# Splitting two more output-gate tiles and interleaving half gate tiles with the attention units of a two-layer hybrid decoder step

## What is computed

```python
h = rmsnorm(x)
hq, hf, hi, hg, nq, kc, vc, ks, vs, kw, vw, ngate, mgate = jnp.split(h @ w_in, splits, axis=-1)
o_hg = hgrn2(hq, hf, hi) * silu(hg)                       # 4 heads, gated by hg
q = rope(nq)                                              # 8 heads of 64, 2 KV groups
o_cmp, o_slc = nsa_cmp_slc(q, ...)                        # compressed blocks, selected blocks
o_win = window(q, ...)                                    # sliding window
o_nsa = g[:, :, 0] * o_cmp + g[:, :, 1] * o_slc + g[:, :, 2] * o_win
mg = sigmoid(mgate)                                       # two merge gates of 1024 channels
x = x + (mg_a * (o_hg @ W_a) + mg_b * (o_nsa @ W_b)) @ w_out
x = x + (gelu(causal_conv3(h2 @ W_gate)) * (h2 @ W_up)) @ W_down,   h2 = rmsnorm(x)
```

## Time and profile before

| | |
|---|---|
| median of 3 runs | 1149.6 us (1146.79 to 1154.12) |
| profiled execution, its own time | 1147.22 us |
| its span | 1145.4 us (1.8 us less than its time) |
| mean granted clock | 0.983 |
| the stage in layer 0 | 143.7 to 244.2 us of the span |
| the same in layer 1 | 699.8 to 800.3 us |

### The profile page before, as it was taken

One profiled execution on the slowest core, in us unless ns is written; L12 is line 12 of the kernel. 1 busy time (PEld: TensorE's weight loads), 2 busy tenths in 40 slices (PEclk: granted clock), 3 DMA queues, 4 the chain that ended last, 5 costly groups with the idle time before them and its releaser, 6 DMA issues.

```text
span 1145.4 us, 21244 instructions
## 1 busy us (share of the span) xinstructions
PE 1111.0 (97%) x8581; PEld 1030.6 (90%) x8581; DVE 726.4 (63%) x1303; ACT 540.3 (47%) x865; POOL 293.0 (26%) x428
## 2 busy tenths in 40 slices
PE   6999999999999999999999999999999999999997
PEld 5988767778999999999999787777899999999996
DVE  5797166557567777763478845565756677777443
ACT  4543265554356555542454335654534555555332
POOL 2156453423121000000024572622311211000002
PEclk8999989999999999999999999899999999999998
DMA  9565322347644444345455635212784444443321
GB/s 295 154 166 207 111 84 75 111 119 221 223 147 148 148 147 148 113 139 170 148 120 197 200 94 164 74 38 76 221 268 148 147 152 154 154 132 120 134 81 47
DMA packets 151752, 165.94 MB, mean 145 GB/s; under 512 B 31596, under 2 KB 114406, under 8 KB 151398
## 3 DMA queue, kind: packets, MB, share of 16 engines
q1 hardware_dynamic: 151654, 164.58, 46.2%
HBM read 156.16 MB, written 12.46 MB: 147 GB/s over the span
## 4 chain that ended last, share of the span: by engine, by line
PE 87%; DVE 8%; ACT 3%; issue 1%; DMA 1%; SPq 0%; DVEq 0%; ACTq 0%
PE mm L707 62%; PE ax L707 22%; PE ax L710 3%; ACT mixb L1353 1%; DVE ring_low L1716 1%; DMA ring<-in_state_conv 1%; DVE mixb L1888 1%; ACT work L1353 1%; ACT attb L1353 1%; DVE wt L2091 0%; DVE mx L2077 0%; DVE sm L1824 0%; DVE mixb L2063 0%; DVE work L2094 0%; DVE sm L2088 0%
## 5 line engine op out<-in xcount | busy, mean ns | idle before, releaser
L1716 DVE TENSOR_TENSOR ring_low<-ring,work_parts 128x2048 fp32r<-128x2048 f32 (+2 forms) x116 | 257.8, 2224 | 132.3 <-ACT work_parts L1353 131.9
L707 PE MATMUL mm<-h_low,work_parts 128*128 128x320 f32 x1072 | 334.8, 312 | 0.0
L707 PE MATMUL mm<-work_parts 128*128 128x320 f32 (+1 forms) x960 | 304.0, 317 | 6.6 <-DVE h_low L1710 4.3
L1353 ACT ACTIVATE work_parts<-ring 128x2048 fp32r<-128x2048 f32 (+2 forms) x116 | 211.7, 1827 | 153.3 <-PE mm L707 82.7
L707 PE MATMUL mm<-work_parts,ring_low 128*128 128x320 f32 x896 | 276.4, 308 | 0.0
L707 PEld LDWEIGHTS mm<-h_low,work_parts 128*128 128x128 f32 x1072 | 202.7, 189 | 0.3
L707 PEld LDWEIGHTS mm<-work_parts 128*128 128x128 f32 x960 | 181.0, 189 | 10.8 <-issue 4.9
L707 PE MATMUL mm<-act_parts,ring_low 128*128 128x320 f32 x576 | 180.0, 312 | 0.0
L707 PE MATMUL mm<-act_parts,work_parts 128*128 128x320 f32 x656 | 173.6, 312 | 0.0
L707 PEld LDWEIGHTS mm<-work_parts,ring_low 128*128 128x128 f32 x896 | 169.1, 189 | 0.0
L707 PE MATMUL ax<-act_parts,work_parts 128*128 128x320 f32 x544 | 126.2, 310 | 0.6 <-DVE ring L2141 0.6
(11 more groups left out here) (256 smaller groups left out, 1762.9 us busy)
## 6 DMA issues: line engine op xcount, KB each, us to landing
ring<-in_w_gate_up SPq DMA_DIRECT2D x44, 1024.0 KB, 6.7
ring<-in_w_in SPq DMA_DIRECT2D x10, 2048.0 KB, 9.0
ring<-in_w_in SPq DMA_DIRECT2D x18, 1024.0 KB, 6.5
ring<-in_w_down SPq DMA_DIRECT2D x8, 1536.0 KB, 6.7
ring<-in_w_out SPq DMA_DIRECT2D x4, 2048.0 KB, 14.0
ring<-in_w_down SPq DMA_DIRECT2D x4, 2048.0 KB, 8.1
ring<-in_w_in SPq DMA_DIRECT2D x32, 128.0 KB, 3.7
ring<-in_cache_cmp_kv SPq DMA_DIRECT2D x32, 128.0 KB
```

The lines of the kernel that those rows point to most:

```text
L707: return nc.tensor.matmul(out, lhsT, rhs, start=start, stop=stop)
L1353: return nc.scalar.activation(out, in_, f, **kw)
L1716: V.tensor_tensor(unit_of(u, ring_r), unit_of(u, ring), unit_high(u).bitcast(F32), ALU.subtract).then_inc(*st.up(w_low[l]))
```

## The change

1. `hg1` and `hg2` join `GATE_TILES` and are computed in parts on PE (24 matmuls each). POOL splits four more half tiles; the first three high parts get buffers of their own (so six halves before the first reuse), POOL begins without waiting for `krt3`, and makes `h_low` after `hg0` and not after `hg2`.
2. PE's order round the prompt units is changed: half tiles (or two steps of one) stand between scores, transposes and values.
3. DVE: `compressed_reduce` is split in `compressed_take` (before unit 0's maxima) and the rest (behind them); `unit_scale(0)` goes ahead of `compressed_scale`; `unit_scale(1)` behind `unit_reduce(2)`. ACT: `unit_exp(0)` ahead of the compressed exponential, sigmoids of `hg0` and `hg1` ahead of `turned(0)`.
4. `max_ready` is raised twice for a prompt unit, after two heads each, and ACT begins with the first two.
5. Samples in pairs: both scores, both reductions, both exponentials, both scalings, then transposes and values; the merge sigmoids come behind the pair. Two more small buffers (`snewTs`, `scmpTs`) allow it. Merge steps are dealt out anew: 27, 9, 3 steps x matmuls of three, and so on.

The names `mm` and `ax` in the rows are the PSUM groups, `act_parts` and `work_parts` the high parts, `ring_low` the low parts of weights, `attb` and `mixb` hold the probabilities of even and odd units.

The diff, cut. Tables, banks and buffers:

```diff
-GATE_TILES = ["hg3"] + [f"mg{y}{m}" for m in range(4) for y in "ab"]
-GATES = [[(1, 0), (1, 1), (2, 0)], [(2, 1), (3, 0), (3, 1)]]
+GATE_TILES = ["hg1", "hg2", "hg3"] + [f"mg{y}{m}" for m in range(4) for y in "ab"]
+GATES = [[(1, 1), (2, 0)], [(2, 1), (3, 0), (3, 1)]]
...
-        out += [(f"tps{n}", "V"), (f"tpn{n}", "A"), (f"ov{n}", "V"), (f"tps{n + 1}", "V"), (f"tpn{n + 1}", "A"),
+        out += [(f"tps{n}", "V"), (f"tpn{n}", "A"), (f"tps{n + 1}", "V"), (f"tpn{n + 1}", "A"), (f"ov{n}", "V"),
                 (f"ov{n + 1}", "V")] + ([("ovt1", "V")] if hb else [])
...
-        half_high = [part(*at, 512).rearrange("p (k c) -> p k c", k=4) for at in ((act_r, 6640), (act_r, 7152), (work_r, 6280))]
+        half_high = [part(*at, 512).rearrange("p (k c) -> p k c", k=4) for at in (
+            (work_r, 7048), (work_r, 7560), (work_r, 8072), (act_r, 6640), (act_r, 7152), (work_r, 6280))]
```

On PE, the prompt units:

```diff
                 scores(0)
-                out_gate(1, l)
+                gate_tile("hg1")
                 scores(1)
-                out_gate(2, l)
+                gate_tile("hg2")
                 turned(0)
+                gate_tile("hg3", 0, 4)
                 scores(2)
+                gate_tile("hg3", 4, KD)
                 values(0)
-                gate_tile("hg3")
+                gate_tile("mga0", 0, 2)
                 turned(1)
-                gate_tile("mga0")
+                gate_tile("mga0", 2, KD)
                 values(1)
                 turned(2)
+                gate_tile("mgb0", 0, 4)
                 scores(3)
-                gate_tile("mgb0")
+                gate_tile("mgb0", 4, KD)
                 values(2)
+                gate_tile("mga1")
```

On PE, the samples:

```diff
                     sample_scores(n, hb, 0)
-                    merge_products(hb, 0 if hb else 3, 8 if hb else 7)
                     sample_scores(n + 1, hb, 1)
+                    merge_products(hb, 0, 9)
                     sample_turned(n)
-                    merge_products(hb, 8 if hb else 10, 7)
+                    merge_products(hb, 9, 3)
+                    sample_turned(n + 1)
                     sample_values(n, hb, 0)
-                    sample_turned(n + 1)
-                    merge_products(hb, 15 if hb else 17, 7)
+                    merge_products(hb, 12, 1)
                     sample_values(n + 1, hb, 1)
                     if hb:
-                        merge_products(1, 22, 2)
+                        merge_products(1, 13, 11)
```

On DVE, the maxima of a prompt unit, in the loop over its heads:

```diff
-                    ve.wait_ge(*st.settled())
-                    V.tensor_scalar(nm[:, 4:12], mx[:, 4:12], -SCALE, None, ALU.mult).then_inc(*st.up(max_ready[L]))
+                        if e % 2:
+                            ve.wait_ge(*st.settled())
+                            mx2, nm2 = (x[:, 4:12].rearrange("p (w e) -> p w e", w=2)[:, :, e - 1:e + 1] for x in (mx, nm))
+                            V.tensor_scalar(nm2, mx2, -SCALE, None, ALU.mult).then_inc(*st.up(max_ready[L]))
```

On DVE, the order:

```diff
+                compressed_take()
+                unit_reduce(0)
                 compressed_reduce()
-                unit_reduce(0)
+                unit_scale(0)
                 compressed_scale()
                 unit_reduce(1)
-                unit_scale(0)
+                unit_turned(0)
+                out_gate(0)
+                unit_reduce(2)
                 unit_scale(1)
```

On DVE, the samples:

```diff
                     sample_reduce(n)
+                    sample_reduce(n + 1)
                     sample_scale(n, 0)
-                    sample_reduce(n + 1)
+                    sample_scale(n + 1, 1)
                     sample_turned(n)
-                    sample_scale(n + 1, 1)
+                    sample_turned(n + 1)
```

On POOL:

```diff
-                po.wait_ge(*AXR[L].filled("krt3"))
                 for n in range(3):
                     high_of_gates(n)
                     low_of_gates(n)
-                po.wait_ge(*MM[L].filled("hg2"))
+                po.wait_ge(*MM[L].filled("hg0"))
```

More of the change, by code:

```diff
@@ L365, in hybrid_step @@
         sprobTs = [part(*at, 512).rearrange("p (x c) -> p x c", x=4) for at in ((attb, 1920), (work, 1920))]
-        snewT = part(attb, 2560 + 4 * T, 384).rearrange("p (x c) -> p x c", x=3)
+        snewTs = [part(attb, at, 256).rearrange("p (x c) -> p x c", x=2) for at in (2560 + 4 * T, 4352)]
+        scmpTs = [part(attb, 4096, P), part(work, 2432, P)]
         orow = part(attb, 4224, P)
@@ L797, in gate_tile @@
                         pe.wait_ge(n_lo, KD * L + k + 1)
-                    last = split_products(bank[:, 0:T], half_high[half % 3][:, kk, :], gate_half(half, ring_r)[:, kk, :],
+                    last = split_products(bank[:, 0:T], high_half(half)[:, kk, :], gate_half(half, ring_r)[:, kk, :],
                                           n_high[k], h_low[:, k, :], k == 0, k == KD - 1)
@@ L958, in merge_products @@
             def merge_products(hb, at, n):
-                for g in range(3):
+                for g in range(len(GATES[hb])):
                     first, end = max(at - KD * g, 0), min(at + n - KD * g, KD)
@@ L1240, in layer @@
                         values(3)
+                    else:
+                        merge_products(0, 13, 3)
                     pe.wait_ge(*AXR[L].emptied_at(f"skt{hb}_3"))
@@ L1572, in sample_turned @@
                         bank = take(AXR[L], f"tpn{n}")
-                        A(snewT[0:SMP, 0:2, :].rearrange("p x c -> p (x c)"), bank[0:SMP, 0:256], ACT.Copy)
-                        A(snewT[0:NCB, 2, :], bank[0:NCB, 256:384], ACT.Copy).then_inc(*st.up(ax_act[L]))
+                        A(snewTs[n % 2][0:SMP].rearrange("p x c -> p (x c)"), bank[0:SMP, 0:256], ACT.Copy)
+                        A(scmpTs[n % 2][0:NCB, :], bank[0:NCB, 256:384], ACT.Copy).then_inc(*st.up(ax_act[L]))
                     n = 4 + 2 * hb
                     sample_exp(n)
+                    sample_exp(n + 1)
+                    sample_turned(n)
+                    sample_turned(n + 1)
                     if hb == 0:
                         merge_gate(0, 1)
-                    merge_gate(*GATES[hb][0])
-                    sample_exp(n + 1)
-                    sample_turned(n)
-                    merge_gate(*GATES[hb][1])
-                    sample_turned(n + 1)
-                    merge_gate(*GATES[hb][2])
+                        merge_gate(1, 0)
+                        merge_gate(1, 1)
+                    else:
+                        for m, y in [(2, 0)] + GATES[1]:
+                            merge_gate(m, y)
                 sc.wait_ge(*AXR[L].filled("ovt1"))
```

51 lines of the change are left out of this document (27 added, 24 removed).

## The result

The changed kernel took 1141.8 us (median of 8 runs, 1139.97 to 1144.02) beside 1154.0 us of the kernel before on the same chip; the ratio is 0.9908 with an interval of 0.989 to 0.9926. In a second set of runs it took 1142.3 us beside 1150.5, ratio 0.992 (0.9901 to 0.9939). By the ratios the change saves 9 to 11 us, 0.8 to 0.9%, which is just within the 1% that the forecast took for no change (0.16 of its chances). The forecast was 1132 us with a range of 1123 to 1140: the direction was right, the size was too large by more than half, and the time lies just outside the range.

The account below looks back on a forecast made before the run. PE, with 87% of the chain, was taken to bound the kernel; prompts -5.6 and samples -2.5 us made -8.1 a layer, -16.2 for two, from 1147.2 to 1131.0, stated as 1132 us, range 1123 to 1140.

Parts of the forecast that it names:

- Scalings in the samples: Sample pairs: each scaling charged 3.2 us, between the 2.65 and 4.30 seen, as POOL works only part of the time.
- Wait 0.9: Samples: PE waits 0.9 us for each of a pair's two scalings, 3.6 us with both half batches, against 4.3 before.
- with 2.65 throughout it is 1.0: Samples: low bound of PE's waits with both half batches, 1.0 us if every scaling takes 2.65 us.
- The half-rate stretch behind the 1.43 us: Samples: clock loss of 1.5 us behind PE's wait at a sample transpose, expected to go since no wait is as long.
- Tiles: hg1 and hg2 in parts: 3.6 us a tile instead of 4.50, saving 0.9 each, 1.8 us per layer.
- Waits in the prompts: Prompt part: added 0.35 us before the first scores, 0.8 at `turned(0)` and 0.8 at `turned(1)`, per layer.
- The 1.95: Prompt part: PE's wait of 1.95 us before unit 2's scores, ended by DVE, expected to go entirely.
- the half-rate stretch of 3.3: Prompt part: clock loss of 3.3 us (6.6 us at half rate) behind the 1.95 us wait, expected to go with it.
- some 0.5: Prompt part: scores that waited again for banks inside, expected to gain some 0.5 us per layer.
- (a): Rival: sample scalings beside POOL stay at their slowest, samples +1.9 instead of -2.5 us a layer, 1141 us; chance 0.10.
- (b): Rival: the clock falls all the same; both half-rate stretches back 1142 us, one of them 1136 to 1139; chance 0.12.
- (d): Rival: POOL and DVE exclude each other fully, in the prompt softmax and before the first scores; slower, 1162 us; chance 0.04.

Follow-up runs that it names:

- `split_alone`: Kernel before with only hg1 and hg2 computed in parts (their buffers and POOL's order included), every other order as before: 1143.8 us, ratio 0.9944.
- `pool_behind_scaling`: Changed kernel with one edit, POOL splits halves 15 and 19 only when both scalings of the sample pair are done: 1128.2 us, ratio 0.9815.

## Why the prediction was wrong, step by step

*Scalings in the samples.* This step failed: "I take 3.2, nearer the short one, as POOL works for part of the time only", and with it "Wait 0.9" twice. The first scaling of each pair took 4.5 us and the second 1.8; the waits are 2.46 and none instead of 0.9 and 0.9. An average over the two was the wrong thing to form, since POOL's halves are released by the very 27 matmuls that were meant to cover the first scaling. For both half batches that is 4.9 us, where 3.6 was forecast. Nor was the short scaling of the earlier trace rows undisturbed. It, too, had an instruction of three columns beside a POOL subtraction (235.13 to 236.40, kernel before):

```profile
235.51 0.91 DVE L2091 TENSOR_TENSOR wt<-gsel,sm 128x3 f32<-128x3 f32 x1
```

Left alone, the same chain takes 1.8 to 1.9 us. A slip besides: "with 2.65 throughout it is 1.0" should be 1.4 (four waits of 0.35), so the ends -5.1 and 1123 should be -4.7 and about 1124. Nothing hangs on it.

*Clock in the samples.* "The half-rate stretch behind the 1.43 us, 1.5 us, I let go, since no wait is as long": a wait of 2.46 came, and the stretch stayed (1.7 us lost). Together the samples came out 3.0 us a layer worse than the forecast of -2.5: 1.3 by the waits and 1.7 by the clock, which makes +0.5 (the 0.3 at `turned(3)` did go); by windows +0.2.

*Tiles.* `hg1` took 3.71 us from start to start and `hg2` 3.77, against 4.50 and 4.42 before: 1.4 instead of 1.8. The rows show why a block costs more than its matmuls; start, us, what, kernel after:

```profile
150.97 0.72 PE L713 MATMUL ax<-work 64*128 64x128 f32 x10
151.63 0.42 PE L713 MATMUL mm<-act_parts,work_parts 128*128 128x320 f32 x1
151.88 0.31 PE L713 MATMUL mm<-h_low,work_parts 128*128 128x320 f32 x1
```

Wide matmuls follow each other at 0.15 us, but the first behind narrow work takes 0.25, and the last has 0.23 until the next narrow one starts (150.30 to 150.53 behind `hg1`). A block thus costs 0.2 on top, and the change cuts three tiles into six blocks in the prompt part: an estimate of 0.6 a layer, which the forecast had at nothing.

*Waits in the prompts.* The 0.40 before the first scores (0.35 forecast) and the 0.78 at `turned(1)` (0.8) are right. At `turned(0)` it was 1.54 instead of 0.8, the second half behind an `nm` held by POOL. The 1.95 and the half-rate stretch of 3.3 went as forecast, but the stretch goes without the reason given, the missing wait, as `split_alone` shows. Of the "some 0.5" of bank waits nothing was found. Sum: -1.4 - 1.95 - 3.3 + 0.6 + 0.4 + 1.54 + 0.78 = -3.3, by windows -3.5, forecast -5.6.

*Rivals.* What happened in the samples is (a), in place and mechanism. Its 1141 is met (1141.8) partly by luck, since it had the samples 1.9 us a layer worse and the prompts 5.6 better, and by windows it was 0.2 and 3.5. It stood at 0.10, because one of two scalings in the rows was fast. (b) is half right, one stretch stayed. (d) named the mechanism, full blocking, but looked in the prompts for what decides: there five instructions were held by 0.3 to 0.9 us each in the softmax of units 0 to 2, while four held in each first scaling came to 2.7 us at the one place where PE was waiting anyway. Its argument against, that only about six instructions "read two SBUF operands of any length", failed too: of the nine held, seven are TENSOR_SCALAR, some with one input of three or four columns. The cited rule should have had more weight, as the earlier trace rows already had the slow scaling beside POOL.

## What to carry to other kernels

When a chain of short dependent DVE instructions ends a wait, look at POOL in the same microseconds before anything else is moved: if a three-column instruction takes over 0.5 us and ends with a POOL instruction, one wait that holds POOL back may cost nothing. Here it gave 12 us on the changed kernel, more than the whole change, but only 5 in the old order of the samples, where other waits took the place. Price a chain beside POOL instruction by instruction, each with the rest of POOL's running one, not by the mean of two examples. And take a large change apart before its gain is explained: here one part (the split of two tiles) gave as much as it did with the new order round it, which won waits and paid as much in new ones.

## What was not expected of the hardware

In places the granted clock fell to half rate where PE had waited for nothing. In `pool_behind_scaling`, layer 1, a window and PE's rows in it:

```profile
764.30:767.80 3.50, 3.50 (x14) 3.50 (x15) 2.91 (x17) 3.38 (x19) 0.00 (x0) 0.53 0.00 0
```

```profile
760.77 3.44 PE L713 MATMUL ax<-work 64*32 64x256 f32 x56
764.14 0.64 PE L713 MATMUL mm<-act_parts 128*128 128x320 f32 x1
764.58 0.47 PE L713 MATMUL mm<-h_low,act_parts 128*128 128x320 f32 x1
```

PE is busy without a gap, with the samples' narrow scores, and the wide matmuls behind them run at 0.27 us each instead of 0.15 (starts 764.58 and, two on, 765.11): 3.5 us at 0.53 lose 1.6. The same place in layer 0 of the same run is at 1.00. In both profiles of the version with POOL placed and maxima in halves, layer 1 has three such stretches and no wait of PE in the whole stage, and layer 0 has none. The profile of the old order with the split, the pairs and POOL's move has four, the one with POOL placed as well has none. The changed kernel had two in the stage in one profile (1140.2 us) and three in the other (1142.8 us). Those without a wait ahead of them begin mostly behind a row of narrow products from 64 channels: the samples' scores, 56 matmuls in 3.4 us, or the compressed scores. But the same row stands at other places without a fall, so this is a pattern in the rows and no cause shown. A forecast that books a stretch at half rate to one wait, as mine did, can be right in size and wrong in cause; what decides whether the clock falls is left open.
